# Gate ranks from raw weights in four column strips with the first head's queries turned between them, and score tiles in two halves of 320 columns

## The chip, the cores and the metric

One Trainium2 chip, one of its cores. The metric is the device time of one execution in microseconds, the median of several runs. The engines are PE (TensorE: matrix products and transposes), DVE (VectorE), ACT (ScalarE), POOL (GpSimd) and SP (SyncE, which only issues transfers); each works through its own instructions in order, and semaphores order them against each other.

## What is computed

One inference step of a two-layer mixer with 512 latent and 128 context tokens, width 2048, all in float32. Each layer projects the modulated tokens once, and feeds attention, a short convolution and a gated linear recurrence (GLA) from the pieces:

```python
proj = xn @ w_in
aq, ak, av, ag, ch, cb, cc, cg, gq, gk, gv, gg, glr = jnp.split(proj, SPLIT_POINTS, axis=-1)
q = rmsnorm(aq.reshape(b, t, ATT_HEADS, HEAD_DIM), q_norm_w)
k = rmsnorm(ak.reshape(b, t, ATT_KV_HEADS, HEAD_DIM), k_norm_w)
...
s = jnp.einsum('bqkgd,bskd->bkgqs', qblk.astype(jnp.float32), kf) * scale
p = jax.nn.softmax(s, axis=-1)
...
lr = glr.reshape(b, t, 2, GLA_RANK)
logits = jnp.einsum('btzr,zrk->btzk', lr, a_up) + a_bias
logf = jax.nn.log_sigmoid(logits.astype(jnp.float32)) / GLA_TAU
```

Latent tokens attend to 640 keys: 512 latent and 128 cached ones. There are 8 query heads, and 2 key and value heads. The last 32 columns of `w_in` (`glr`, 2 directions of 16) give the gate ranks.

## The kernel before

**Layout.** Activations lie with features on the 128 partitions and the 640 tokens (`TOK`) along the row; the 2048 features are `KT` = 16 slices. To keep float32 accuracy in fast matmuls, an operand is split into a rounded part and its rest (`x_high`, `x_low`; `high`, `low` for weights, split by ACT and DVE), and each product is three matmuls: high by high, high by low, low by high. Of 640 columns each is made in two halves of `HALF` = 320, since a PSUM bank holds 512; the result starts at column `AT` = 192 of a two-bank tile, so that the halves meet at the bank border.

**Order within a layer.** All order is written out by hand, one stream per engine. First the front: `w_in` in 64 chunks for most projections (L732, L742), with key norms and modulation weights in between. Then `project_quarter(0, 0)` (L767), a first piece of the convolution's projections, which go on in quarters through all attention heads. Then the last prompt turn (`turn_prompt`, L755), whose result ACT stores to the scratch `proj_dram` (L1210), and `gate_ranks` (L693): for each of the 16 slices three products, each in two halves, with 32 weight columns of interest in a block of 128. Its weights came into `raw[1]` by SP (`LR_SLOT`), and DVE splits them (`lr_split`). ACT copies the 32 result rows out (L1298) and stores them.

**The fence.** Between front and heads all engines pass a fence; ACT only once its stores have landed. SP then loads in order: cached key and value tile (L453, L454), tables `cos` and `sin`, the query rows of head 0 into `qraw` (whose memory is named `rstd`, L480), and four partition-swapped pieces into `qturn` (L483). `q_in` counts all five query loads.

**A head.** PE transposes keys and values once per group (L888 to L891), and for each head the raw queries (L925) into `psP[1]`; ACT squares them (L1318), from which DVE gets the norm factors. DVE rotates the queries (L1806 to L1816). PE makes four score tiles of 128 queries by 640 keys (L904) and one small prompt tile (L907); behind each, DVE takes the row maximum (L1845), ACT the exponential (L1329), DVE scales, PE turns the probabilities (L915). Between the tiles PE works on a quarter of a projection. A product with the values (L946) ends the head. For the first head the function `head_products` is called with `begun=True`, since its first quarter has been done.

**The gate logits.** After the heads, and behind a second fence and an output block (`fill`, L973), PE multiplies the stored ranks with `gla_a_up` (L637). `gate_in` loads the ranks (L529) and the two directions' weights (L531) into `aup`, which DVE has cleared before (L1880). It is called twice per layer.

Of the kernel before, what the change touches and what calls it, by code (L numbers as in the profile page):

```python
# [18 lines left out]
F32 = mybir.dt.float32  # L19
F32R = mybir.dt.float32r  # L20
ALU = mybir.AluOpType
# [3 lines left out]
P = 128  # L25
# [114 lines left out]
LR_SLOT = 1  # L140


# [36 lines left out]
mod_step0 mod_step1 mod_half mod_acc mod_summed lr_in lr_split lr_done old_in0 old_in1 x_sq x_acc k_in v_in  # L179
# [18 lines left out]
def backbone(nc, io):  # L198
    with ExitStack() as ctx:
# [42 lines left out]
        with ExitStack() as proj_space:  # L242
# [4 lines left out]
            with ExitStack() as mixers:  # L247
# [15 lines left out]
                lr = lr_att[0:LR_W, :]  # L263
                aup = mx("aup", [LR_W, 2, P])
# [76 lines left out]
        q_back = psP[1][:, 0:TOK]  # L341
# [26 lines left out]
        def _(sp):  # L368
# [46 lines left out]
            for l in range(DEPTH):  # L415
# [10 lines left out]
                for n in range(RING, FRONT_CHUNKS):  # L426
# [7 lines left out]
                    if n == K_LOAD:  # L434

                        sp.wait_ge(s["x_saved"], 16 * SAVES * (l + 1))
# [197 lines left out]
        def _(pe):  # L634
# [190 lines left out]
            for l in range(DEPTH):  # L825
# [50 lines left out]
                pe.wait_ge(s["lr_split"], 2 * l + 2)  # L876
                pe.wait_ge(s["mod_taken"], MOD_CHUNKS + (l + 1) * UNITS + SEED)
                pe.wait_ge(s["k_roped"], (l + 1) * KVH)
                gate_ranks()
                pe.wait_ge(s["prompt_back"], (l + 1) * len(FRONT))  # L880
                for g in range(KVH):
# [12 lines left out]
                    def head_products(h, begun=False):  # L894
# [3 lines left out]
                        def score(i):  # L898

                            pe.wait_ge(s["probs_made"], hd * TT + i + SEED)  # L900
                            if i < TT - 1:
                                for q, x in ((q_high, k_high), (q_high, k_low), (q_low, k_high)):
                                    for part in (slice(0, DEC), slice(DEC, KEYS)):
                                        mm = pe.matmul(psP[1][:, part], q[:, i * P:(i + 1) * P], x[:, part],  # L904
                                                       start=(q is q_high and x is k_high), stop=(q is q_low))
                            else:
                                mm = pe.matmul(psP[1][:, 0:SEQ], qw[:], key[:, g, DEC:TOK], start=True, stop=True)  # L907
# [12 lines left out]
                        else:  # L920
                            pe.wait_ge(s["lr_done"], 2 * l + 2)
                        pe.wait_ge(s["q_in"], hd * 80 + 80)
                        pe.wait_ge(s["probs_made"], hd * TT + SEED)
                        for i in range(TT):
                            mm = pe.transpose(q_back[:, i * P:(i + 1) * P], qraw[:, i * P:(i + 1) * P], ident[:])  # L925
                        mm.then_inc(s["q_rot"], 1)
# [16 lines left out]
                        pe.wait_ge(s["gated"], hd + SEED)  # L943
                        for j in range(KEYS // P):
# [65 lines left out]
                for pr in range(PAIRS):  # L1010
# [5 lines left out]
                    pe.wait_ge(s["gla_lr_in"], gp * 16 * 3 + 16 * 3)  # L1016
# [100 lines left out]
        def _(act):  # L1117
# [59 lines left out]
            for l in range(DEPTH):  # L1177
# [113 lines left out]
                for g in range(KVH):  # L1291
# [3 lines left out]
                    act.activation(k_high[:, 0:DEC], key[:, g, 0:DEC], ACT.Copy).then_inc(s["kv_ready"], 1)  # L1295
# [883 lines left out]
```

## Time and profile before

| | |
|---|---|
| median of 3 runs | 2228.21 us (2228.12 to 2229.08) |
| the profiled execution: time, span | 2229.19 us, 2227.4 us |
| PE busy | 2174.2 us, 98% of the span |
| PE weight loads | 1922.4 us, 86% |
| DVE busy | 1381.7 us, 62% |
| ACT busy | 679.4 us, 31% |
| POOL busy | 186.0 us, 8% |
| granted PE clock, mean | 0.994 |

Weight loads run beside matmuls. A busy PE is one with a matmul in flight. Matmuls are pipelined, so the time that one adds is the distance between starts, not its own duration: a row "x2" that lasts 0.46 us may be followed by the next 0.29 us later. In the trace a plain float32 matmul appears as two instructions. Times are microseconds from the span's start.

### The profile page before, as it was taken

Reading aid. Unit: us, or ns where it says so; the run is one execution under the profiler, and the core shown is the slowest. Engines: PE = TensorE matmul, PEld = TensorE weight load, DVE = VectorE, ACT = ScalarE, POOL = GpSimd, SP = SyncE. Lnnn points to the kernel's source line nnn. Section 1 sums busy time; section 2 is a strip of 40 time slices with the busy share of each in tenths; the row PEclk is TensorE's granted clock in tenths of the full one; section 3 lists DMA queues with packets and bytes.
Section 4 is the critical chain, followed back from the end, with each engine's and each line's share of the span. In section 5 each row is a group of like instructions: output and inputs, shape, how many; then the busy total and the mean of one; then the engine's idle time right before and its main releaser. Section 6 shows DMA issues by size and latency. Waiting matters only on the chain.

```text
span 2227.4 us, 34005 instructions
## 1 busy us (share of the span) xinstructions
PE 2174.2 (98%) x13257; PEld 1922.4 (86%) x13257; DVE 1381.7 (62%) x2701; ACT 679.4 (31%) x1196; POOL 186.0 (8%) x125
## 2 busy tenths in 40 slices
PE   5999999999999999999989999999999999999998
PEld 2578877888999999999988888887799999999998
DVE  5469777986565666666457454555446666666654
ACT  4332222321343333533134222232133333344312
POOL 0000000000000000423321000000000000042331
PEclk9999999999999999999989999999999999999999
DMA  9988587664432333664444645444343333366444
GB/s 353 381 299 299 184 262 229 204 212 138 122 104 79 94 101 111 198 195 134 119 135 141 192 139 177 146 127 129 88 128 91 101 100 101 97 197 196 133 123 146
DMA packets 353200, 362.49 MB, mean 163 GB/s; under 512 B 17062, under 2 KB 259580, under 8 KB 352444
## 3 DMA queue, kind: packets, MB, share of 16 engines
q1 hardware_dynamic: 323536, 317.65, 45.8%
q10 hardware_dynamic: 29548, 43.25, 5.4%
q8 instruction: 78, 1.28, 0.2%
q14 instruction: 38, 0.31, 0.0%
HBM read 301.97 MB, written 58.88 MB: 162 GB/s over the span
## 4 chain that ended last, share of the span: by engine, by line
PE 91%; DVE 3%; ACT 2%; DMA 1%; issue 1%; ACTq 0%; SPq 0%; DVEq 0%
PE psP L732 32%; PE psP L767 20%; PE psP L784 10%; PE psT L742 8%; PE psO L973 5%; PE psP L904 3%; PE psO L946 2%; PE psT L915 2%; PE psO L693 1%; PE psT L973 1%; PE psT L650 1%; PE psO L650 1%; PE psO L797 1%; PE psP L985 1%; PE psP L674 1%
## 5 line engine op out<-in xcount | busy, mean ns | idle before, releaser
L732 PE MATMUL psP<-x_high,high 128*128 128x512 f32 x1024 | 413.1, 403 | 5.6 <-DVE x_low L1689 5.0
L732 PE MATMUL psP<-x_high,low 128*128 128x512 f32 x1024 | 400.7, 391 | 0.0
L732 PE MATMUL psP<-x_low,high 128*128 128x512 f32 x1024 | 400.7, 391 | 0.0
L1634 DVE SCALAR_TENSOR_TENSOR macc<-mraw,cond,macc 128x384 f32<-128x384 f32 (+1 forms) x960 | 389.7, 480 | 0.0
L1175 ACT ACTIVATE high<-raw 128x1024 fp32r<-128x1024 f32 x128 | 135.4, 1058 | 520.8 <-PE psT L742 507.0
L732 PEld LDWEIGHTS psP<-x_high,high 128*128 128x128 f32 x1024 | 193.2, 189 | 65.3 <-issue 24.0
L767 PE MATMUL psP<-x_high,high 128*128 128x320 f32 x1024 | 243.3, 319 | 0.5 <-issue 0.5
L767 PE MATMUL psP<-x_high,low 128*128 128x320 f32 x1024 | 233.3, 309 | 0.0
L767 PE MATMUL psP<-x_low,high 128*128 128x320 f32 x1024 | 232.7, 308 | 0.0
L732 PEld LDWEIGHTS psP<-x_high,low 128*128 128x128 f32 x1024 | 193.1, 189 | 41.6
L732 PEld LDWEIGHTS psP<-x_low,high 128*128 128x128 f32 x1024 | 193.5, 189 | 39.0 <-issue 1.9
L1652 DVE TENSOR_TENSOR low<-raw,high 128x1024 fp32r<-128x1024 f32 x128 | 163.9, 1281 | 100.0 <-ACT high L1175 100.0
L767 PEld LDWEIGHTS psP<-x_low,high 128*128 128x128 f32 x1024 | 171.0, 188 | 0.0
L767 PEld LDWEIGHTS psP<-x_high,low 128*128 128x128 f32 x1024 | 170.9, 188 | 0.0
L767 PEld LDWEIGHTS psP<-x_high,high 128*128 128x128 f32 x1024 | 167.1, 189 | 1.5 <-issue 0.7
L973 PE MATMUL psO<-x_high,high 128*128 128x320 f32 x704 | 134.9, 313 | 4.7 <-DVE low L1904 4.7
L2082 POOL MEMSET cu<- 128x643 f32 x2 | 1.3, 636 | 1645.8 <-DVEq L359 1645.8
L784 PE MATMUL psP<-second_high,high 128*128 128x320 f32 x512 | 116.9, 309 | 0.2 <-DVE low L1587 0.2
L973 PEld LDWEIGHTS psO<-x_high,high 128*128 128x128 f32 x704 | 109.2, 188 | 8.8 <-issue 7.4
L784 PE MATMUL psP<-second_low,high 128*128 128x320 f32 x512 | 116.6, 309 | 0.0
L784 PE MATMUL psP<-second_high,low 128*128 128x320 f32 x512 | 116.6, 309 | 0.0
L1624 DVE TENSOR_SCALAR macc<-mraw,cond 128x384 f32<-128x384 f32 (+1 forms) x64 | 19.7, 350 | 156.2 <-PE psO L797 144.7
(312 smaller groups left out, 3508.1 us busy)
## 6 DMA issues: line engine op xcount, KB each, us to landing
raw<-in_w_in_dram SPq DMA_DIRECT2D x128, 512.0 KB, 4.7
wmod<-in_w_mod_dram SPq DMA_DIRECT2D x32, 1024.0 KB, 9.5
mraw<-in_w_mod_dram SPq DMA_DIRECT2D x64, 512.0 KB, 4.3
mraw<-in_w_mod_dram SPq DMA_DIRECT2D x32, 1024.0 KB, 7.0
raw<-in_w_in_dram SPq DMA_DIRECT2D x32, 1024.0 KB, 6.1
raw<-in_w_out_dram SPq DMA_DIRECT2D x64, 512.0 KB, 4.4
old<-x_scratch SPq DMA_DIRECT2D x64, 320.0 KB, 3.0
proj_scratch<-stage ACTq DMA_DIRECT2D x64, 256.0 KB, 3.2
```

Of the source, the lines that this page charges most:

```text
L650: mm = pe.matmul(mod_ps[t % 2][32 * k:32 * k + 2, :], cond[:, q * KT // 4 + k, :], wmod[q][:, k, :], start=(q == 0), stop=(q == 3), skip_g ...
L732: mm = pe.matmul(latent_ps[m], w[:, kk, cols], x[:, k, 0:DEC], start=(k == 0 and w is whole and x is x_high), stop=(k == KT - 1 and w is r ...
L742: mm = pe.matmul(prompt_ps, x[:, k, DEC:TOK], w[:, kk, :], start=(k == 0 and w is whole and x is x_high), stop=(k == KT - 1 and w is rest))
L767: mm = pe.matmul(psP[0][:, AT + half * HALF:AT + (half + 1) * HALF], w[slot][:, k, :], x[:, k, half * HALF:(half + 1) * HALF], start=(k == ...
L784: mm = pe.matmul(out[:, AT + half * HALF:AT + (half + 1) * HALF], w[slot][:, at + k, :], x[:, k, half * HALF:(half + 1) * HALF], start=(k ...
L904: mm = pe.matmul(psP[1][:, part], q[:, i * P:(i + 1) * P], x[:, part], start=(q is q_high and x is k_high), stop=(q is q_low))
L915: mm = pe.transpose(psT[:, j * P:(j + 1) * P], probs[i % 2][:, j * P:(j + 1) * P], ident[:])
L946: pe.matmul(psO[:, 0:DEC], v[:, j, :], x[:, j, :], start=(j == 0 and v is vals_high and x is probs_high), stop=(j == KEYS // P - 1 and v i ...
L973: mm = pe.matmul(out[:, AT + half * HALF:AT + (half + 1) * HALF], w[slot][:, at + k, :], x[:, k, half * HALF:(half + 1) * HALF], start=(k ...
L1175: act.activation(ring(high, n), ring(raw, n), ACT.Copy).then_inc(s["chunk_cast"], 1)
L1634: m = dve.scalar_tensor_tensor(acc[:, v, 0:width], mraw[hf][:, k, 0:width], c, acc[:, v, 0:width], ALU.mult, ALU.add)
L1652: dve.tensor_tensor(ring(low, n), ring(raw, n), ring(high, n).bitcast(F32), ALU.subtract)\
```

## The change

Four things are done in the same edit.

1. The gate rank weights are loaded raw, 32 columns wide, into a place of their own (`lr_w`) in the middle of the front, and are not split. The ranks are plain float32 matmuls against `x_high` and `x_low`. The output goes to four strips of 32 PSUM partitions: slice k + n to strip n. Each strip holds the partial sum of four slices. The four are not added there: all 128 rows are copied, stored and loaded again, and `aup` holds four copies of its 32 rows, so that the gate logits' contraction over 128 rows adds them.
2. The ranks are made in two halves (slices 0 to 7, 8 to 15), and head 0's query turn, taken out of `head_products` as `query_turn`, stands between them. ACT makes head 0's squares ahead of its copy of the ranks. The wait for `lr_done` moves from the head's start to its value product.
3. The score tile goes to `score_ps`, which starts at column 192, in two halves of 320 columns instead of 512 and 128. Row maximum and exponential read it there.
4. SP's load of the second convolution weight slot no longer waits for the rank weights' split.

```diff
+            with ExitStack() as rank_space:
+                ps_("below", [P, KT * MOD_N + 72], F32, rank_space)
+                lr_w = ps_("lr_w", [P, KT, LR_W], F32, rank_space)
...
-        q_back = psP[1][:, 0:TOK]
+        q_back, score_ps = psP[1][:, 0:TOK], psP[1][:, AT:AT + KEYS]
...
                     if n == K_LOAD:
+                        sp.dma_start(lr_w[:], w_in[:, :, T_LR * P:T_LR * P + LR_W]).then_inc(s["lr_in"], 16)
...
                 sp.wait_ge(s["chunk_split"], (l + 1) * FRONT_CHUNKS)
-                sp.dma_start(raw[LR_SLOT][:, :, 0:LR_W], w_in[:, :, T_LR * P:T_LR * P + LR_W]).then_inc(s["lr_in"], 16)
-                sp.wait_ge(s["lr_split"], 2 * l + 2)
                 conv_weights(1, 0)
...
-                    sp.dma_start(lr, proj_dram[T_LR, 0:LR_W, :]).then_inc(s["gla_lr_in"], 16)
-                    for z in range(2):
-                        sp.dma_start(aup[z * RANK:(z + 1) * RANK, z, :], io["gla_a_up"][l, z][:, pr * P:(pr + 1) * P])\
-                            .then_inc(s["gla_lr_in"], 16)
+                    sp.dma_start(lr, proj_dram[T_LR]).then_inc(s["gla_lr_in"], 16)
+                    for at in range(0, P, LR_W):
+                        for z in range(2):
+                            sp.dma_start(aup[at + z * RANK:at + (z + 1) * RANK, z, :],
+                                         io["gla_a_up"][l, z][:, pr * P:(pr + 1) * P]).then_inc(s["gla_lr_in"], 16)
...
-            def gate_ranks():
-                for k in range(KT):
-                    for w, x in ((high, x_high), (high, x_low), (low, x_high)):
+            def gate_ranks(first, last):
+                for k in range(first, last, LR_STRIPS):
+                    for x in (x_high, x_low):
                         for half in range(2):
-                            mm = pe.matmul(lr_ps[:, half * HALF:(half + 1) * HALF], w[LR_SLOT][:, k, :],
-                                           x[:, k, half * HALF:(half + 1) * HALF],
-                                           start=(k == 0 and w is high and x is x_high), stop=(k == KT - 1 and w is low))
-                mm.then_inc(s["lr_done"], 1)
+                            part = slice(half * HALF, (half + 1) * HALF)
+                            for n in range(LR_STRIPS):
+                                mm = pe.matmul(lr_ps[n * LR_W:(n + 1) * LR_W, part], lr_w[:, k + n, :],
+                                               x[:, k + n, part].bitcast(F32), start=(k == 0 and x is x_high),
+                                               stop=(k == KT - LR_STRIPS and x is x_low), skip_group_check=True)
+                if last == KT:
+                    mm.then_inc(s["lr_done"], 1)
+
+            def query_turn(hd):
+                pe.wait_ge(s["q_in"], hd * 80 + 80)
+                pe.wait_ge(s["probs_made"], hd * TT + SEED)
+                for i in range(TT):
+                    mm = pe.transpose(q_back[:, i * P:(i + 1) * P], qraw[:, i * P:(i + 1) * P], ident[:])
+                mm.then_inc(s["q_rot"], 1)
...
-                pe.wait_ge(s["lr_split"], 2 * l + 2)
+                pe.wait_ge(s["lr_in"], 32 * l + 16)
                 pe.wait_ge(s["mod_taken"], MOD_CHUNKS + (l + 1) * UNITS + SEED)
                 pe.wait_ge(s["k_roped"], (l + 1) * KVH)
-                gate_ranks()
+                gate_ranks(0, KT // 2)
+                query_turn(l * HEADS)
+                gate_ranks(KT // 2, KT)
...
-                                    for part in (slice(0, DEC), slice(DEC, KEYS)):
-                                        mm = pe.matmul(psP[1][:, part], q[:, i * P:(i + 1) * P], x[:, part],
+                                    for part in (slice(0, HALF), slice(HALF, KEYS)):
+                                        mm = pe.matmul(score_ps[:, part], q[:, i * P:(i + 1) * P], x[:, part],
...
+                    def query_squares(hd):
+                        act.wait_ge(s["q_rot"], hd + 1 + SEED)
...
                     if g == 0:
+                        query_squares(hd0)
                         act.wait_ge(s["lr_done"], 2 * l + 1)
-                        act.activation(stage[0][0:LR_W, :], lr_ps[0:LR_W, :], ACT.Copy).then_inc(s["lr_done"], 1)
+                        act.activation(stage[0][:], lr_ps, ACT.Copy).then_inc(s["lr_done"], 1)
...
-                dve.tensor_copy(high[LR_SLOT][:, :, 0:LR_W], raw[LR_SLOT][:, :, 0:LR_W]).then_inc(s["lr_split"], 1)
-                dve.wait_ge(s["lr_split"], 2 * l + 1)
-                dve.tensor_tensor(low[LR_SLOT][:, :, 0:LR_W], raw[LR_SLOT][:, :, 0:LR_W],
-                                  high[LR_SLOT][:, :, 0:LR_W].bitcast(F32), ALU.subtract).then_inc(s["lr_split"], 1)
...
-                        dve.wait_ge(s["lr_done"], 2 * l + 1)
```

PE's queue in layer 0, around the ranks, before (`psO<-x_high,high` are the ranks, `psT<-ident,r_b` the last prompt turn, `psP<-x_low,high` the projection):

```order
L767 MATMUL psP<-x_high,low 128x320 x2
L755 MATMUL psT<-ident,r_b 128x128 [waits prompt_back,prompt_taken]
L755 MATMUL psT<-ident,r_b 128x128 x3
L693 MATMUL psO<-x_high,high 128x320 [waits k_roped,mod_taken,lr_split]
L693 MATMUL psO<-x_high,high 128x320
L693 MATMUL psO<-x_low,high 128x320 x2
L693 MATMUL psO<-x_high,low 128x320 x2
```

and the same place of the changed kernel, to the key and value turns (`psT<-ident,xf`, `psT<-ident,ck`); `psP<-ident,rstd` is the query turn:

```order
L768 MATMUL psT<-ident,r_b 128x128 [waits prompt_back,prompt_taken]
L768 MATMUL psT<-ident,r_b 128x128 x3
L697 MATMUL psO<-x_high,lr_w 32x320 [waits k_roped,mod_taken,lr_in]
L697 MATMUL psO<-x_high,lr_w 32x320 x7
L697 MATMUL psO<-x_low,lr_w 32x320 x8
L697 MATMUL psO<-x_high,lr_w 32x320 x8
L697 MATMUL psO<-x_low,lr_w 32x320 x8
L708 MATMUL psP<-ident,rstd 128x128 [waits probs_made,q_in]
L708 MATMUL psP<-ident,rstd 128x128 x4
L697 MATMUL psO<-x_high,lr_w 32x320 x8
L697 MATMUL psO<-x_low,lr_w 32x320 x8
L697 MATMUL psO<-x_high,lr_w 32x320 x8
```

Before, 96 matmuls stood in one piece; now 32 stand ahead of the wait for `q_in` and 32 behind it.

SP's queue between the front and the heads, before:

```order
L395 DMA raw<-in_w_in_dram 128x2x512 [waits chunk_split]
L459 DMA raw<-in_w_in_dram 128x16x128 [waits split0,chunk_split]
L448 DMA xf<-proj_scratch 128x640 [waits kv_turned]
L466 DMA raw<-in_w_in_dram 128x16x32 [waits chunk_split]
L459 DMA raw<-in_w_in_dram 128x16x128 [waits split1,lr_split]
L453 DMA ck<-in_cache_k_dram 128x128 [waits phase_over]
```

The rank weight load (L466) is gone from here, and the load behind it waits for `chunk_split` alone. At the gate logits the changed kernel's SP queue reads:

```order
L530 DMA lr_att<-proj_scratch 128x640 [waits aup_clear]
L533 DMA aup<-in_gla_a_up_dram 16x128 x8
L545 DMA states<-in_state_gla_dram 128x128 [waits phase_over]
L545 DMA states<-in_state_gla_dram 128x128
```

where there were two `aup` loads, and the first load had 32 rows.

## Rows read from the trace of the kernel before

**Rows 1.** The page, chain of work that ended last, shares of the span by engine
```profile
PE 91%; DVE 3%; ACT 2%; DMA 1%; issue 1%; ACTq 0%; SPq 0%; DVEq 0%
```

**Rows 2.** Timeline of PE, layer 0, ranks to first head: start us, us, engine, instruction
```profile
555.19 0.54 PE L693 MATMUL psO<-x_high,high 128*128 128x320 f32 x2
...
569.57 0.71 PE L891 MATMUL psT<-ident,xf 128*128 128x128 f32 x5
...
570.82 0.54 PE L767 MATMUL psP<-x_high,high 128*128 128x320 f32 x2
```

**Rows 3.** Timelines of SP, ACT and DVE there; last: DMA issues, median us to landing
```profile
551.90 0.37 SPq L459 DMA_DIRECT2D raw<-in_w_in_dram  x1
...
556.16 0.39 ACTq L1210 DMA_DIRECT2D proj_scratch<-r_a  x1
...
559.68 0.34 SPq L453 DMA_DIRECT2D ck<-in_cache_k_dram  x1
...
567.65 0.29 DVE L1806 TENSOR_SCALAR qw<-rstd,vecs 128x128 f32<-128x128 f32 x1 [2.74 <-DMA qturn<-proj_scratch]
...
proj_scratch<-r_a ACTq DMA_DIRECT2D x16, 256.0 KB, 2.5
```

**Rows 4.** Timeline of PE, conditioning matmuls in four column strips
```profile
102.59 1.90 PE L650 MATMUL psT<-wmod,cond 128*2 128x512 f32 x16
...
106.01 1.04 PE L650 MATMUL psT<-wmod,cond 128*2 128x512 f32 x8
```

**Rows 5.** Windows (us; PE, PEld, DVE, ACT, POOL busy; PEclk; DMA); then timeline of PE
```profile
1148.00:1150.00 2.00, 1.42 (x6) 1.42 (x7) 0.46 (x3) 0.00 (x0) 0.00 (x0) 0.52 0.00 0
...
1160.00:1162.00 2.00, 2.00 (x7) 1.51 (x6) 1.97 (x5) 1.15 (x2) 0.00 (x0) 0.57 0.71 152
...
1156.10 0.76 PE L732 MATMUL psP<-x_high,high 128*128 128x512 f32 x1 [5.02 <-DVE x_low L1689]
```

**Rows 6.** Timelines of DVE and PE, layer 0, head 0
```profile
575.76 0.17 DVE L1826 TENSOR_SCALAR qv<-qb 128x5 f32<-128x5 f32 x1 [1.56 <-ACT probs L1318]
...
576.86 0.51 PE L767 MATMUL psP<-x_high,high 128*128 128x320 f32 x2
...
577.21 0.46 PE L767 MATMUL psP<-x_low,high 128*128 128x320 f32 x2
...
580.76 0.56 PE L904 MATMUL psP<-k_high,q_high 128*128 128x512 f32 x2 [0.16 <-ACT probs L1329]
```

**Rows 7.** Timeline of PE, one score tile of a later query tile
```profile
590.67 0.46 PE L767 MATMUL psP<-x_high,low 128*128 128x320 f32 x2
...
590.96 0.45 PE L904 MATMUL psP<-k_high,q_high 128*128 128x512 f32 x2
...
591.25 0.51 PE L904 MATMUL psP<-k_low,q_high 128*128 128x512 f32 x2
...
591.60 0.51 PE L904 MATMUL psP<-k_high,q_low 128*128 128x512 f32 x2
...
591.94 0.71 PE L915 MATMUL psT<-ident,probs 128*128 128x128 f32 x5
```

**Rows 8.** Timelines of SP and PE, first gate logits; last: DMA issues
```profile
884.65 0.33 SPq L529 DMA_DIRECT2D lr_att<-proj_scratch  x1
...
885.01 0.89 SPq L531 DMA_DIRECT2D aup<-in_gla_a_up_dram  x2
...
888.93 1.12 PE L637 MATMUL psP<-lr_att,aup 32*128 32x512 f32 x2
...
aup<-in_gla_a_up_dram SPq DMA_DIRECT2D x8, 8.0 KB, 2.1
```

**Rows 9.** Timelines of DVE and PE, layer 1, same places as rows 2, 3, 6
```profile
1630.80 0.28 DVE L1806 TENSOR_SCALAR qw<-rstd,vecs 128x128 f32<-128x128 f32 x1 [1.86 <-DMA qturn<-proj_scratch]
...
1634.40 0.54 PE L767 MATMUL psP<-x_high,high 128*128 128x320 f32 x2
...
1644.32 0.57 PE L904 MATMUL psP<-k_high,q_high 128*128 128x512 f32 x2 [0.16 <-ACT probs L1329]
```

More of the change, by code:

```diff
@@ L902, in score @@
                                 for q, x in ((q_high, k_high), (q_high, k_low), (q_low, k_high)):
-                                    for part in (slice(0, DEC), slice(DEC, KEYS)):
-                                        mm = pe.matmul(psP[1][:, part], q[:, i * P:(i + 1) * P], x[:, part],
+                                    for part in (slice(0, HALF), slice(HALF, KEYS)):
+                                        mm = pe.matmul(score_ps[:, part], q[:, i * P:(i + 1) * P], x[:, part],
                                                        start=(q is q_high and x is k_high), stop=(q is q_low))
                             else:
-                                mm = pe.matmul(psP[1][:, 0:SEQ], qw[:], key[:, g, DEC:TOK], start=True, stop=True)
+                                mm = pe.matmul(score_ps[:, 0:SEQ], qw[:], key[:, g, DEC:TOK], start=True, stop=True)
                             mm.then_inc(s["scored"], 1)
@@ L919, in head_products @@
                             project_quarter(0, 0, n)
[L920 to L926, printed above, removed]
+                            query_turn(hd)
                         project_quarter(0, 1, n)
@@ L1295, in _ @@
                     act.activation(k_high[:, 0:DEC], key[:, g, 0:DEC], ACT.Copy).then_inc(s["kv_ready"], 1)
+                    def query_squares(hd):
+                        act.wait_ge(s["q_rot"], hd + 1 + SEED)
+                        for i in range(TT):
+                            act.activation(q_squares[:, i * P:(i + 1) * P], q_back[:, i * P:(i + 1) * P], ACT.Square,
+                                           accum_out=qb[:, i:i + 1]).then_inc(s["q_sq"], 1)
                     if g == 0:
+                        query_squares(hd0)
                         act.wait_ge(s["lr_done"], 2 * l + 1)
[L1298 removed]
+                        act.activation(stage[0][:], lr_ps, ACT.Copy).then_inc(s["lr_done"], 1)
                         act.wait_ge(s["lr_done"], 2 * l + 2)
[L1300 removed]
+                        act.dma_start(proj_dram[T_LR], stage[0][:]).then_inc(s["lr_in"], 16)
                     act.wait_ge(s["kv_turned"], kv + 1 + SEED)
@@ L1313, in _, with head_scalars @@
                                   newv[:]).then_inc(s["kv_stored"], 16)
-                    def head_scalars(h):
+                    def head_scalars(h, squared=False):
                         hd = h + hd0
-                        act.wait_ge(s["q_rot"], hd + 1 + SEED)
-                        for i in range(TT):
-                            act.activation(q_squares[:, i * P:(i + 1) * P], q_back[:, i * P:(i + 1) * P], ACT.Square,
-                                           accum_out=qb[:, i:i + 1]).then_inc(s["q_sq"], 1)
+                        if not squared:
+                            query_squares(hd)
                         act.wait_ge(s["q_r"], hd + 1)
@@ L1328, in prob @@
                             act.wait_ge(s["prob_turned"], hd * TT + max(i - 1, 0) + SEED)
-                            act.activation(probs[i % 2][:, 0:width], psP[1][:, 0:width], ACT.Exp,
+                            act.activation(probs[i % 2][:, 0:width], score_ps[:, 0:width], ACT.Exp,
                                            bias=nm[:, i:i + 1], scale=qs[:, i:i + 1], accum_out=sums[:, i:i + 1])\
@@ L1362, in head_scalars @@
                         take_tile(1)
-                    with act.Fori(0, GROUP) as h:
+                    if g == 0:
+                        head_scalars(0, squared=True)
+                    with act.Fori(1 if g == 0 else 0, GROUP) as h:
                         head_scalars(h)
```

17 lines of the change are left out of this document (9 added, 8 removed).

## The prediction

> **What bounds the kernel now.** I read the page's chain of work first: 91% of the span is PE's own work, so time is won or lost where PE's own stream gets shorter or where PE comes to stand still [rows 1]. Then the timeline of the stretch between the front projection and the first attention head, PE alone. In layer 0 the gate ranks (L693) begin at 555.19, the key and value turns (L891) at 569.57, the first head's projection (L767) at 570.82 [rows 2]. The ranks are 96 matmuls of 320 columns at about 0.147 us (a pair takes 0.29, [rows 7]): 14.1 us of the stream.
>
> Next, what the other engines and queues do beneath those 14 us [rows 3]. The last prompt store leaves ACT's queue at 556.16; ACT passes the fence only when it has landed, and SP's first load behind the fence is issued at 559.68. Then come two cache tiles, two tables, the query row tile and its four turned parts, one behind another, and DVE's first query step (L1806) begins at 567.65, released by the last of them. So the query of head 0 is there 12.5 us after the ranks begin. Now that costs nothing: PE needs it only at 570.3. The 14.1 us of ranks are the cover of this load chain, and that is what the reader should carry into the next part.
>
> **Part 1: the ranks in strips.** 64 matmuls per layer, four at a time in four column strips. The nearest rows are the conditioning matmuls (L650): the same strips, the same 128 rows, plain float32, 512 columns, but 2 weight columns. Each shows as two instructions; 16 take 1.90 us and 8 take 1.04 [rows 4], so 8 more cost 0.86 us, which is a set of four matmuls. For 320 columns that is 0.54 us a set, 16 sets a layer: 8.6 us, 4.3 a half. Weight loads have 32 columns here instead of 2; what they add is not in the rows. I take 4.4 us a half. Upper bound, if the strips do not run together: 64 times 0.54 is 34 us.
>
> By the Trainium skill, page "TensorE: Matmul & The Clock Gate" (Part 3, The mechanism), weight loads pass running matmuls only where the row group differs, and all four strips share their rows; with that page's 27 ns for 32 columns, an estimate of 1.7 us more for each half. No row here shows it.
>
> **Part 2: the query turn between the halves.** It waits for all of q_in, and in PE's queue the second half of the ranks, the key and value turns and the head's projection stand behind it. The first half ends at 555.2 + 4.4 = 559.6. The query is due at 567.65 as before, or sooner: SP used to issue a 1 MB weight load at 551.90, held back until the rank weights were split, and the prompt store ran beside it and took 3.5 us to the fence, where the median of such stores is 2.5 [rows 3]. That load now goes out earlier. I take 0.9 us for this (bounds 0 and 1.3): query at 566.75. So PE stands still for about 7 us, and the shorter ranks win nothing: the load chain sets the restart.
>
> What follows the restart: five query turns and seven key and value turns, 1.5 us (the ranks end near 569.35, 96 times 0.1475 after 555.19, and L767 begins at 570.82, [rows 2]), and 4.4 us of ranks, 5.9 us at full clock. The clock will not be full, I think. In the longest gap of this trace the granted clock reads 0.52 (the 1.2 GHz level) in the window 1148 to 1150, where PE does thin work with pauses; then PE idles 5.02 us, restarts at 1156.10, and in the window 1160 to 1162 the clock still reads 0.57, so it rose near 1161.7, some 5.4 us after the restart [rows 5]. With the same here, the first 5.4 us do 2.7 us of work: L767 begins at 566.75 + 5.4 + 3.2 = 575.35, 4.5 us later than before. With the clock full it would be 572.65.
>
> Part of that comes back. Before, DVE waited 1.56 us for ACT's query squares, and score 0 with it; the squares are now made long before. Score 1 started at 580.76, released by ACT's first exponential [rows 6]. From the end of the key and value turns (570.28, [rows 2]) to that release there lie 10.5 us on ACT and DVE; less the 1.56, 8.9. The new turns end at 575.3, so score 1 starts at 584.2; PE itself would be there at 583.3. **Layer 0: +3.4 us.** In layer 1 the query came 3.60 us before L767 (1630.80, 1634.40), in layer 0 3.17 us [rows 2, 3, 9], so its shift is 0.4 smaller: **+3.0 us**. Its score 1 was at 1644.32, with the same 0.16 us wait [rows 9], so the tail is the same.
>
> **Part 3: the score halves.** 8 heads, 4 tiles, 2 layers: 64 tiles of three pairs, 512 + 128 columns before, 320 + 320 now. In a steady head the pair before the score starts at 590.67 and the score at 590.96; the next pairs at 591.25 and 591.60, the probability turns at 591.94 [rows 7]. So a 512 + 128 pair costs 0.35 behind another such pair, and all three 0.98 us. A pair of 320s costs 0.293; three are 0.88. That saves 0.10 a tile. Where a projection follows instead of a turn, its first pair takes 0.35 instead of 0.29 (576.86 to 577.21, [rows 6]): 0.06 more, for tile 0 of each head. Both heads of the chain above already hold their own tile 0, so 48 tiles at 0.10 and 14 at 0.16: **-7.0 us**. No wait stands between the rows of a steady head, so PE's shorter stream counts in full. Bounds: 0, and 0.057 on all 192 pairs, 10.9 us.
>
> A rule speaks against this term. The Trainium skill, same page (Wait — 56ns, not 53.3ns?), puts the gap between matmuls at N / 2.4 GHz + 2.5 ns: 271.6 ns for either pair, so the halves would win nothing. The 0.35 of the rows does not agree with it, and the measured pairs go into the sum.
>
> **Part 4: the low-rank weights in four copies.** SP issues nine loads instead of three before the gate logits (L637). Before: first at 884.65, the next two from 885.01 in 0.89 us, 0.445 each; logits at 888.93, straight behind a fill [rows 8]. Now the last of eight starts at 888.1 and lands 2.1 us later, at 890.2: PE stops for **1.3 us**, in both layers, +2.6. The state loads behind them in SP's queue come later too; I take them as covered by the later logits. The second pair's loads start 20 us before their use and cost nothing; the eight cost nothing there. The contraction over 128 rows instead of 32 streams the same columns. If small loads landed at once, 0; if as slowly as 4 us, 3.2 a layer.
>
> **Part 5, at nothing:** the two split steps that DVE loses, which PE does not wait for; the 256 KB rank weight load moved into the front, one SP issue under PE's front work; the 128-row copy and store instead of 32 rows.
>
> **Sum.** +3.4 + 3.0 - 7.0 + 2.6 = +2.0 us. The profiled execution took 2229.19 us, span 2227.4, 1 us above the median of 2228.21; on the median the sum gives **2230.2**. No change that a measurement of this kernel can tell begins at about 0.2%, 4.5 us.
>
> **The rivals.**
> *The clock holds, or the query comes much sooner.* Part 2 then ends at 572.65 for L767, and score 1 at 570.28 to 572.6 shifted: 572.6 + 8.9 = 581.5, +0.7 us instead of +3.4, and +0.3 in layer 1. Sum -3.4; with logits that do not stall, or scores at their upper bound, -6 to -7: 2221 to 2224. For it: PE idles 7 us, not longer, and only one gap bears the clock out. Against: that gap was shorter. 0.28, about half of it beyond 4.5 us below.
> *The strips do not overlap at 32 columns* (slower). Half the ranks then take 17 us: the first half covers the query, the second ends at 589.4 and L767 starts near 590.9, 20 us late; with 1.6 won back at the score it is +18 a layer: 2265. Against: [rows 4]. It decides once a set costs more than about 0.8 us instead of 0.54. 0.06.
> *The small loads land late* (a dearer wait than the one I forecast). If each takes 4 us from issue to landing instead of 2.1, the logits wait 3.2 us a layer, +3.8 in all: 2234. Their transfers share the queue with a 320 KB load ahead of them, which speaks for it; the median of eight speaks against. 0.14.
> *The halves win nothing* (the page's rule): pairs of equal column count, 640, would take equal time, as they would if the 0.06 us were lost elsewhere. Sum +9.0: 2237. 0.07, since [rows 7] speak against it.
> My own case: 0.45.
>
> **How the numbers follow.** Range 2222 to 2237: from the middle of the first rival to the fourth, leaving the strips' failure and the best sums out. Faster by over 0.2%: half or more of the first rival and the upper tail of Part 3, 0.24. Slower: strips, late loads above the bound, no gain of the halves, and a slice of my own case, 0.26. Between, 0.50.
>
> **What would show it.** A PE gap of about 7 us ahead of the query turn in both layers, released by the turned query parts; a granted clock of 0.5 in the windows after it and rank matmuls there at twice the spacing; each layer's rank matmuls busy for 4 to 5 us a half at full clock; score 1 of head 0 some 3 us later than before, counted from the ranks' start; score tiles of 0.88 us from first matmul to the turn; a wait of about 1.3 us ahead of the first gate logits in each layer on the eighth small load. I am wrong if the query arrives by 562, if the clock stays full through the gap, or if the score tile keeps 0.98.

## The result and the profile after

The changed kernel took 2232.96 us (median of 16 runs, 2229.47 to 2237.83), the kernel before 2228.28 us on the same chip (16 runs): ratio 1.0023, 95% interval 1.0016 to 1.0030. That is 3.6 to 6.7 us slower, 5.1 in the middle, against a forecast of 2.0.

The profiled execution took 2229.47 us, which is the shortest of its 16 runs. I therefore read places and mechanisms from it, and sizes also from a second profile of the same kernel (experiment 1, 2232.88 us, near the median). First the page of the changed kernel: engines, and the chain that ended last.

```profile
PE 2156.2 (97%) x13321; PEld 1902.7 (85%) x13321; DVE 1378.4 (62%) x2697; ACT 669.2 (30%) x1188; POOL 186.4 (8%) x125
...
PE 22%; DVE 2%; ACT 1%; issue 1%; DMA 1%; SPq 0%; ACTq 0%; DVEq 0%
```

The chain's shares add up to 27% of the span; the view follows the chain over a much shorter way than in [rows 1], so the two can't be set against each other. That PE is busy 97% of the span still says where to look: at the places where it stands still. Its waits in the changed kernel (total us, times, longest):

```profile
PE psP L708 <- DMA qturn<-proj_scratch: 12.2, 2, 6.5
...
PE psP L919 <- ACT probs L1346: 2.9, 2, 1.4
...
PE psP L639 <- DMA aup<-in_gla_a_up_dram: 2.7, 2, 1.8
```

The first and the last of these are new. The middle one stood at 0.16 a layer before [rows 6]. Next, PE's timeline in layer 0 from the ranks (L697) past the turn (L708) to the first head (L780), the counterpart of [rows 2]:

```profile
553.87 1.28 PE L697 MATMUL psO<-x_high,lr_w 128*32 128x320 f32 x16
...
554.97 1.26 PE L697 MATMUL psO<-x_low,lr_w 128*32 128x320 f32 x16
...
564.90 1.33 PE L708 MATMUL psP<-ident,rstd 128*128 128x128 f32 x5 [6.52 <-DMA qturn<-proj_scratch]
566.16 2.36 PE L697 MATMUL psO<-x_high,lr_w 128*32 128x320 f32 x16
568.29 1.61 PE L697 MATMUL psO<-x_low,lr_w 128*32 128x320 f32 x16
569.73 1.25 PE L697 MATMUL psO<-x_high,lr_w 128*32 128x320 f32 x16
...
572.27 0.71 PE L906 MATMUL psT<-ident,xf 128*128 128x128 f32 x5
572.73 0.54 PE L780 MATMUL psP<-x_high,high 128*128 128x320 f32 x2
...
582.33 0.56 PE L919 MATMUL psP<-k_high,q_high 128*128 128x320 f32 x2 [1.44 <-ACT probs L1346]
```

Each row of 16 instructions is a group of eight matmuls. The groups begin 1.10, 1.08 and 1.07 us apart, so a half of the ranks, four groups, is 4.3 us. Then PE stands 6.52 us. The first group after the restart takes 2.13 us until the next, twice as long, the second 1.44, and the third has the old pace. The windows show the clock there (us; PE, PEld, DVE, ACT, POOL busy; PEclk; DMA), as [rows 5] did:

```profile
559.00:561.00 2.00, 0.00 (x0) 0.00 (x0) 0.00 (x0) 0.00 (x0) 0.00 (x0) 1.00 0.92 283
561.00:563.00 2.00, 0.00 (x0) 0.00 (x0) 0.84 (x2) 0.00 (x0) 0.00 (x0) 0.80 0.88 272
563.00:565.00 2.00, 0.10 (x1) 0.10 (x2) 0.12 (x1) 0.00 (x0) 0.00 (x0) 0.50 0.98 275
...
567.00:569.00 2.00, 2.00 (x20) 0.76 (x16) 1.34 (x3) 0.67 (x6) 0.00 (x0) 0.50 0.56 134
569.00:571.00 2.00, 2.00 (x36) 0.87 (x32) 0.00 (x0) 0.00 (x0) 0.00 (x0) 0.99 0.00 0
```

The granted clock falls to 0.50, the 1.2 GHz level, while PE stands idle, and is back at 2.4 GHz about 4 us after the restart at 564.90. What the query waits for stands on ACT, SP and DVE, the counterparts of [rows 3]:

```profile
554.66 0.39 ACTq L1221 DMA_DIRECT2D proj_scratch<-r_a  x1
...
557.11 0.34 SPq L458 DMA_DIRECT2D ck<-in_cache_k_dram  x1
...
564.88 0.28 DVE L1820 TENSOR_SCALAR qw<-rstd,vecs 128x128 f32<-128x128 f32 x1 [2.49 <-DMA qturn<-proj_scratch]
```

From the issue of the prompt store (554.66) to SP's first load behind the fence (557.11) there are 2.45 us (3.52 before), and the query is there 11.0 us after the ranks begin (12.5 before). Behind it, the first head's exponential on ACT:

```profile
580.01 1.28 ACT L1346 ACT_TABLE_LOAD   x1 [2.89 <-DVE nm L1861]
581.31 0.89 ACT L1346 ACTIVATE probs<-psP,nm,qs 128x640 f32<-128x640 f32 x1
```

The table load of 1.28 us starts only after DVE's last maximum step (`nm`), so all of it lies open: from the end of `nm` to the start of the exponential there are 1.37 us. In the kernel before it started at 578.43, after the step before the maximum (`qs`), and 0.33 us lay open. In the changed kernel head 0 stands outside ACT's loop over the heads; the 14 heads inside it still have the load behind `qs`. A steady score tile and the gate logits, on PE's timeline, counterparts of [rows 7] and [rows 8]:

```profile
592.33 0.46 PE L919 MATMUL psP<-k_high,q_high 128*128 128x320 f32 x2
...
593.21 0.71 PE L930 MATMUL psT<-ident,probs 128*128 128x128 f32 x5
...
888.89 1.12 PE L639 MATMUL psP<-lr_att,aup 128*128 128x512 f32 x2 [1.76 <-DMA aup<-in_gla_a_up_dram]
```

And the nine small loads ahead of these logits, on SP's timeline:

```profile
882.76 0.33 SPq L530 DMA_DIRECT2D lr_att<-proj_scratch  x1
883.13 3.67 SPq L533 DMA_DIRECT2D aup<-in_gla_a_up_dram  x8
```

The tile takes 0.88 us where it took 0.98, and the logits wait 1.76 us for the eighth load; in layer 1 they wait 0.9.

### The profile page after: what moved, and what is told of

It reads as the page before. It is cut to its first block and busy times, and to the rows that moved or that the text cites. A ratio compares the mean times of both kernels' runs of the same rounds, so it can differ in the third digit from the quotient of the medians.

```text
span 2227.6 us, 34115 instructions
## 1 busy us (share of the span) xinstructions
PE 2156.2 (97%) x13321; PEld 1902.7 (85%) x13321; DVE 1378.4 (62%) x2697; ACT 669.2 (30%) x1188; POOL 186.4 (8%) x125
## 5 line engine op out<-in xcount | busy, mean ns | idle before, releaser
L780 PE MATMUL psP<-x_high,high 128*128 128x320 f32 x1024 | 242.6, 318 | 0.5 <-issue 0.5
L780 PE MATMUL psP<-x_high,low 128*128 128x320 f32 x1024 | 233.3, 309 | 0.0
L780 PE MATMUL psP<-x_low,high 128*128 128x320 f32 x1024 | 232.9, 309 | 0.0
L780 PEld LDWEIGHTS psP<-x_low,high 128*128 128x128 f32 x1024 | 171.2, 188 | 0.0
L780 PEld LDWEIGHTS psP<-x_high,low 128*128 128x128 f32 x1024 | 170.9, 188 | 0.0
L780 PEld LDWEIGHTS psP<-x_high,high 128*128 128x128 f32 x1024 | 167.5, 188 | 0.8 <-issue 0.6
L984 PE MATMUL psO<-x_high,high 128*128 128x320 f32 x704 | 134.9, 313 | 6.2 <-DVE low L1917 6.2
L984 PEld LDWEIGHTS psO<-x_high,high 128*128 128x128 f32 x704 | 109.2, 188 | 10.4 <-issue 9.0
```

What stands on the lines that cost most here:

```text
L780: mm = pe.matmul(psP[0][:, AT + half * HALF:AT + (half + 1) * HALF], w[slot][:, k, :], x[:, k, half * HALF:(half + 1) * HALF], start=(k == ...
L984: mm = pe.matmul(out[:, AT + half * HALF:AT + (half + 1) * HALF], w[slot][:, at + k, :], x[:, k, half * HALF:(half + 1) * HALF], start=(k ...
```

## The experiments

Each ratio is to the kernel before on the same chip. Experiments 1 to 4 shared one chip (before: 2227.39 us, 13 runs), 5 to 8 another (2228.26 us, 27 runs).

**1. The changed kernel again**, no edit.

> The changed kernel once more, beside the others on the same chip. My theory (PE stands still before the query turn, the clock falls, and how long it stays low differs from run to run): 2229 to 2236 us, and the executions lie wider apart than those of the kernel before; the mean granted clock is lower where the time is longer, near 0.988 at the slow end and 0.992 at the fast end. Rival (the change costs a fixed 4 to 5 us, and the spread is chance): times within 1 to 2 us of 2233, and no tie between clock and time.

2233.47 us, ratio 1.0025 (1.0014 to 1.0036). The eight runs lie between 2230.19 and 2236.07 us, the 13 of the kernel before between 2226.62 and 2229.47; the longest has the lowest mean clock (0.989) and the shortest one of the highest (0.992), as expected. Its layer 1 on PE's timeline, and then two windows there:

```profile
1629.13 1.33 PE L708 MATMUL psP<-ident,rstd 128*128 128x128 f32 x5 [5.67 <-DMA qturn<-proj_scratch]
1630.39 2.36 PE L697 MATMUL psO<-x_high,lr_w 128*32 128x320 f32 x16
1632.53 2.36 PE L697 MATMUL psO<-x_low,lr_w 128*32 128x320 f32 x16
1634.66 1.50 PE L697 MATMUL psO<-x_high,lr_w 128*32 128x320 f32 x16
...
1647.51 0.57 PE L919 MATMUL psP<-k_high,q_high 128*128 128x320 f32 x2 [1.44 <-ACT probs L1346]
```

```profile
1633.00:1635.00 2.00, 2.00 (x20) 0.79 (x16) 0.00 (x0) 0.00 (x0) 0.00 (x0) 0.50 0.00 0
1635.00:1637.00 2.00, 2.00 (x32) 0.72 (x24) 0.00 (x0) 0.00 (x0) 0.00 (x0) 0.96 0.00 0
```

Here two groups and part of a third run at the low level: the clock came back some 6 us after the restart. In the shortest run the same layer had waited as long (5.69 us) and was back about 3 us after. The gap hardly differs; how long the clock stays low does, and with it the time from run to run. The same shows where no edit reaches: behind the wait of 5.02 us in [rows 5] the clock came back 5.6 us after the restart (1156.10 to about 1161.7), and behind the same wait of 5.01 us in experiment 1 after 3.0 (1157.67 to about 1160.7):

```profile
1160.00:1162.00 2.00, 2.00 (x9) 1.62 (x8) 2.00 (x2) 1.78 (x4) 0.53 (x1) 0.83 0.95 356
```

**2. The halves alone**, on the kernel before:

```diff
-for part in (slice(0, DEC), slice(DEC, KEYS)):
-    mm = pe.matmul(psP[1][:, part], ...
+for part in (slice(0, HALF), slice(HALF, KEYS)):
+    mm = pe.matmul(score_ps[:, part], ...      # score_ps = psP[1][:, AT:AT + KEYS]
...                                              # maximum and exponential read score_ps
```

> The kernel before with the score tiles in two halves of 320 columns and nothing else. My theory: 48 + 14 tiles at 0.10 and 0.16 us, and two more tiles 0 that the wait for the squares does not hide: 6.5 to 7.3 us faster than before, about 2221.3. Rival (equal columns take equal time): 2228, no change.

2221.30 us, ratio 0.9969 (0.9957 to 0.9981): 4.2 to 9.6 us faster, 6.9 in the middle (6.1 between the medians). From head 0's to head 7's value matmuls in layer 0 there are 269.58 us where before had 272.75; seven heads at 0.46 should save 3.22, and 3.17 was saved.

**3. Everything but the halves**, on the changed kernel:

```diff
-score_ps = psP[1][:, AT:AT + KEYS]
+score_ps = psP[1][:, 0:KEYS]
-for part in (slice(0, HALF), slice(HALF, KEYS)):
+for part in (slice(0, DEC), slice(DEC, KEYS)):
```

> The changed kernel with its score tiles in 512 + 128 columns again, so the ranks, the query turn and the four copies alone. My theory: 7 us slower than the changed kernel, 2237 to 2243, that is 9 to 14 us slower than before. Rival (the halves win nothing, or the ranks' part is worth a gain): 2226 to 2233.

2240.75 us, ratio 1.0060 (1.0046 to 1.0074), 10.2 to 16.5 us slower, 13.4 in the middle, where the terms gave 9.0. The granted clock of its profiled run also drops behind the logits' wait:

```profile
895.00:897.00 2.00, 2.00 (x6) 0.97 (x5) 0.00 (x0) 0.79 (x1) 0.00 (x0) 0.50 0.92 296
```

From there to the second pair's logits it needs 77.23 us, the kernel before 75.16. So a wait of 1.8 us at the logits can cost some 2 us more behind it. In the profiles of the changed kernel (both) the clock held there, and that stretch took 75.12 and 75.46 us.

**4. The ranks in one piece**, the query turn back in front of its head, and ACT's squares back in its loop over the heads:

```diff
-gate_ranks(0, KT // 2)
-query_turn(l * HEADS)
-gate_ranks(KT // 2, KT)
+gate_ranks(0, KT)
...
-    query_squares(hd0)                          # ACT, ahead of its copy of the ranks
...
-    head_scalars(0, squared=True)
-with act.Fori(1 if g == 0 else 0, GROUP) as h:
+with act.Fori(0, GROUP) as h:
```

> The changed kernel, but the 16 slices of the ranks in one piece and the query turn behind the key and value turns, as before. My theory: ranks end near 8.7 us after they begin, PE waits only 1 to 3 us for the query instead of 6.5, the ranks' second half stands ahead of the wait and at full clock; first head 5 to 8 us earlier per layer: 12 us faster than the changed kernel, about 2221 (2216 to 2225), and close executions if the clock stays full. Rival (the place of the query turn does not matter, the loads behind the fence or the strips themselves set the time): 2230 to 2236.

2220.15 us, ratio 0.9964 (0.9951 to 0.9978). PE's timeline in layer 0, then a window there, then ACT's timeline:

```profile
562.43 1.26 PE L697 MATMUL psO<-x_low,lr_w 128*32 128x320 f32 x16
...
563.90 0.71 PE L904 MATMUL psT<-ident,xf 128*128 128x128 f32 x5
566.53 0.77 PE L708 MATMUL psP<-ident,rstd 128*128 128x128 f32 x5 [1.93 <-DMA qturn<-proj_scratch]
...
576.61 0.56 PE L917 MATMUL psP<-k_high,q_high 128*128 128x320 f32 x2
```

```profile
568.00:570.00 2.00, 2.00 (x10) 2.00 (x9) 1.90 (x5) 1.99 (x11) 0.00 (x0) 0.50 1.09 349
```

```profile
574.28 1.28 ACT L1343 ACT_TABLE_LOAD   x1 [1.87 <-DVE qs L1847]
```

With all ranks and the key and value turns ahead of it, the same query costs 1.93 us of waiting instead of 6.66. Score 1 starts 22.3 us after the last prompt turn, in experiment 1 29.2, in the kernel before 25.9. The difference is 6.9 us in layer 0 and 7.2 in layer 1, against 13.6 us between this kernel and the changed one (ratios: 0.0061). About 1 us of it in each layer is not the place of the turn: ACT's table load is behind `qs` again, and the exponential starts 0.35 us after `nm` and not 1.37. The clock falls here too, behind the wait of 1.93 us, but for a shorter time.

Against experiment 2, which has the halves and no strips, this kernel is only 0.0005 (1 us) faster, and the intervals overlap. Score 1 comes 3.7 and 4.1 us earlier than in the kernel before, but part of that is lost again behind the heads, 2.6 us in the waits at the logits alone. So with the turn in its old place the strips win nothing that these runs can tell; with the turn between their halves they lose.

**5. Work in the gap**, 27 matmuls that nothing reads, ahead of the turn:

```diff
 gate_ranks(0, KT // 2)
+pe.wait_ge(s["probs_made"], l * HEADS * TT + SEED)
+for _ in range(27):
+    pe.matmul(psP[1][:, 0:DEC], high[1][:, 0, :], x_high[:, 0, 0:DEC], start=True, stop=True)
 query_turn(l * HEADS)
```

> The changed kernel with 27 extra matmuls of 512 columns, about 6.1 us, in PE's wait between the first half of the ranks and the query turn; their output is overwritten and belongs to nothing. My theory (the clock falls in the gap and the restart pays for it at 1.2 GHz): the granted clock stays full there, the second half takes 4.4 us instead of 5.4 to 6.5, 2 to 3 us per layer come back, so 4 to 6 us faster than the changed kernel, 2228 to 2230, and executions closer together, mean clock 0.994. Rival (only the wait itself costs): no faster than 2233, or slower by what the filler overhangs.

2230.43 us, ratio 1.0012 (1.0003 to 1.0022). PE's timeline, and then two windows:

```profile
559.06 6.46 PE L895 MATMUL psP<-x_high,high 128*128 128x512 f32 x27
565.36 0.71 PE L708 MATMUL psP<-ident,rstd 128*128 128x128 f32 x5
...
570.61 0.27 PE L907 MATMUL psT<-ident,ck 128*128 128x128 f32 x1
...
1972.21 0.82 PE L987 MATMUL psO<-x_high,high 128*128 128x320 f32 x4 [1.87 <-DVE low L1920]
```

```profile
567.00:569.00 2.00, 2.00 (x37) 0.93 (x31) 1.66 (x3) 0.50 (x4) 0.00 (x0) 1.00 0.80 197
888.00:890.00 2.00, 2.00 (x5) 1.10 (x4) 0.00 (x0) 0.46 (x1) 0.00 (x0) 0.50 0.84 255
```

The clock stays at 1.00, and from the turn to the first cache turn PE needs 5.25 us; experiment 1 needed 7.3 in layer 0 and 8.2 in layer 1. So the low clock costs 2.1 and 2.9 us in the two layers of experiment 1. Of those 5.0 us the ratios show 2.9 (0.0013), with an uncertainty as large. In layer 1 little of it can be seen even in the profile: there the query came 12.3 us after the ranks began, where experiment 1 had 10.2, so PE stood 1.43 us behind the 27 matmuls, and score 1 came only 0.8 us earlier than in experiment 1 (2.5 in layer 0). SP's issue of the `cos` table took 1.48 us there and not 0.43, and the parts landed later; whether the extra matmuls have to do with it stays open. In the profiled run the clock fell at two other places: behind the logits' wait in layer 0 (window 888 to 890), and in layer 1 behind a wait of 1.87 us for a split (L987, last row; 0.75 in the kernel before). From the first to the second pair's logits that run needs 76.75 and 77.59 us in the two layers, experiment 1 75.46 and 75.78: 3.1 us given back.

**6. One copy instead of four.** It leaves out three of the four copies, so the gate logits take the first strip's partial sum alone and the outputs are not those of the step; only its time is of use.

```diff
-LR_LOADS = 1 + 2 * LR_STRIPS
+LR_LOADS = 3
-for at in range(0, P, LR_W):
+for at in (0,):
```

> The changed kernel with two of the eight loads of low-rank weights in each gate load; it leaves out three of the four copies, so the gate logits take the first strip's partial sum alone. My theory: the waits of 1.8 and 0.9 us ahead of the first gate logits vanish, and the later loads of that stage come 2.7 us earlier, 2.7 us in all: 2229.5 to 2231.5. Where the stage loses more than the two waits, as the fills behind seem to (6.3 us of waits on weight splits against 4.7 before), up to 5 us: 2228. Rival (the extra small loads are hidden): 2233.

2230.12 us, ratio 1.0008 (0.9999 to 1.0017). No wait stands ahead of the logits any more. The four copies cost the difference to experiment 1, 0.0017 or 3.8 us. That is uncertain by some 3 us, so it agrees with the 2.6 us of their two waits and shows no more.

**7. The ranks in one piece and the copies loaded early**: experiment 4, and a tile of its own for all pairs' copies, loaded during the front.

```diff
+if n in range(40, 40 + PAIRS):
...
+    for at in range(0, P, LR_W):
+        for z in range(2):
+            sp.dma_start(aups[at + z * RANK:at + (z + 1) * RANK, n - 40, z, :],
+                         io["gla_a_up"][l, z][:, (n - 40) * P:(n - 39) * P]).then_inc(s["aups_in"], 16)
...
```

> The ranks in one piece with the query turn behind the key and value turns, as in e4, and the four copies of the low-rank weights loaded in the front into a place of their own, so that the gate logits wait for one load only. My theory: e4's 2220.2 less the stall and what follows it, 2.7 to 4 us: 2216 to 2217.5. Rival (the sixteen small loads in the front delay its weight chunks, or the stall is not what the stage loses): 2219 to 2222.

2215.98 us, ratio 0.9947 (0.9934 to 0.9961), the fastest kernel here with experiment 9: 0.0022 or 4.9 us better than the halves alone, 3.8 better than experiment 4 (the middles of overlapping intervals). The logits follow a fill without a wait, and PE's wait for the query is short, once a layer (PE's timeline; then its waits: total, times, longest):

```profile
879.98 1.02 PE L645 MATMUL psP<-lr_att,aups 128*128 128x512 f32 x2
```

```profile
PE psP L714 <- DMA qturn<-proj_scratch: 3.2, 2, 1.9
```

**8. The turn waits for the raw query alone**, not for its four turned parts:

```diff
-pe.wait_ge(s["q_in"], hd * 80 + 80)
+pe.wait_ge(s["q_in"], hd * 16 + 16)        # the turned parts count on qt_in, for DVE
```

> The changed kernel, but the query turn waits only for the raw query rows, not for the four turned pieces, which have a semaphore of their own. My theory (the load chain behind the fence sets the restart): the query turn starts 1.5 to 2.5 us sooner, the gap shrinks from 6.5 to about 4.5 us in layer 0, and 3 to 5 us are won in all: about 2229. Rival (the transfers all end together, since the later ones share the queues): the turn starts less than 0.7 us sooner, 2232.

2229.84 us, ratio 1.0009 (1.0000 to 1.0018). PE's timeline:

```profile
564.22 1.33 PE L708 MATMUL psP<-ident,rstd 128*128 128x128 f32 x5 [5.52 <-DMA rstd<-proj_scratch]
```

The raw query itself comes late: 5.52 us of the gap stay. What the parts add is 1.1 us in this layer and 0.6 in the other, so the expected step of 1.5 to 2.5 us did not come, though the time of 2229 nearly did. Score 1, counted from the last prompt turn, comes 1.7 and 2.0 us earlier than in experiment 1; in layer 1 0.6 of that is the wait, and the rest is a clock that came back 3.4 us after the restart and not 6.0.

**9. Experiments 7 and 8 together** (a chip with before at 2228.50 us, 9 runs).

> e7 with the query turn waiting for the raw query rows alone, as in e8. In e7 PE waited 3.2 us in two places for the turned pieces, and in layer 0 the granted clock fell for a short stretch behind that wait. My theory: the raw rows land 0.7 to 1 us sooner, so 1.5 to 2 us of the waits go, and the score that follows now waits for DVE, whose own query steps still need the turned pieces; 0 to 2 us faster than e7, 2214 to 2216. Rival (DVE's rotated queries set the first score anyway): 2216, no change.

2215.86 us, ratio 0.9940 (0.9926 to 0.9953), not to be told from experiment 7. Waits of PE:

```profile
PE psP L923 <- DVE vals_low L1814: 3.3, 2, 1.6
...
PE psP L714 <- DMA rstd<-proj_scratch: 1.6, 2, 0.9
```

The wait moved: PE turns the query earlier and then stands at the first score for DVE's split of the values.

## Why the prediction came out as it did

The time fell inside the range and on the forecast side of zero, 3 us above the forecast. The forecast steps were there, but the sum left 3 us out, and the width of the range covered them; "within 0.2%" was the likeliest of three, and the ratio of 1.0023 lies just beyond it. The account below is made in the profile of experiment 1 against that of before: spans 2231.1 and 2227.4, +3.7 us.

**Part 1, right.** 4.4 us a half was forecast and 4.3 measured. The Trainium skill, page "TensorE: Matmul & The Clock Gate" (Part 3, The mechanism), would have added an estimated 1.7 us a half, since strips that share their rows can't load weights under running matmuls; the 1.08 us for each 16 instructions do not agree: they are 0.54 for a set of four matmuls, what the rows of the conditioning matmuls gave without such a term.

**Part 2, right in kind and in sum.** The gap was forecast at about 7 us, released by the turned parts, and was 6.52 and 5.69 us (6.66 and 5.67 in experiment 1). The store passed the fence 1.07 us sooner; 0.9 was taken for the whole chain, and the query came 11.0 us after the ranks' start (11.2 in experiment 1) where 11.6 was forecast. The clock was forecast to stay low for 5.4 us after the restart and stayed low for 3 to 6. That figure came from one gap, misread twice: by [rows 5] it is 5.6 us (1156.10 to 1161.7), and that gap is not the longest of the trace, since PE waits 13.66 us at its start. Errors inside cancel, which is luck: the low clock cost 1.4 to 2.9 us where 2.7 was taken; the query came up to half a microsecond sooner than taken; and from the key and value turns to score 1 there lie 9.6 us (572.73 to 582.33) where 8.9 was taken, because ACT's table load, for the most part under DVE's row maximum before, now comes after it. Counted from the last prompt turn, score 1 of experiment 1 is 3.3 us later than before in layer 0 and 3.2 in layer 1, where +3.4 and +3.0 were forecast. Experiment 5 says how much of that is the clock (2.1 and 2.9 us). With the turn in its old place (experiment 4) score 1 is not later but 3.7 and 4.1 us earlier than before; about 1 us of that turnabout is the table load, the rest is the place of the turn.

**Part 3, right.** 0.88 us a tile, 3.17 us over seven heads, and 6.9 us in all (4.2 to 9.6) for a forecast of 7.0. The Trainium skill, same page (Wait — 56ns, not 53.3ns?), has a gap that depends on columns alone and would give nothing for the halves; the 0.98 and 0.88 us don't agree with it.

Parts 2 and 3 together, from the last prompt turn to head 7's value matmuls, were to give -0.1 us in layer 0 and -0.5 in layer 1. They gave -0.21 and -0.30.

**Part 4, the size right, a consequence missing.** The logits wait 1.7 and 0.9 us in experiment 1, 2.6 in all, as forecast (1.3 in each). The missing step is that the clock can fall behind a wait of this kind. It did so in experiments 3 and 5, in layer 0, where 2.1 and 1.6 us were lost up to the next pair, and not in the four other profiles that have the wait. The prediction saw the clock at risk in the long gap only. The trace of the kernel before had a warning: among the conditioning matmuls at its start, with waits of 1.40 and 1.58 us (47.26 and 49.88), the clock fell too (window, as [rows 5]):

```profile
50.00:52.00 2.00, 2.00 (x9) 0.30 (x2) 1.97 (x3) 1.66 (x4) 0.00 (x0) 0.50 1.05 386
```

Since the profiles of the changed kernel itself don't have the drop at the logits, how often its other runs have it stays open. Experiment 3 lies 4.4 us above its terms, but the changed kernel lies 3.1 and 3.6 above its own (ratios 1.0023 and 1.0025), so that excess is for the most part not this drop.

**What the sum left out.** The terms give +2.1 in that profile, the span grew by 3.7. Of the rest, 1.3 us stand at the very end. The DMA engines' mean busy share and GB/s in the last 4.4 us, 40 slices, in the kernel before and then in the changed one:

```profile
DMA  9999979989979899989899999997997700000000
GB/s 410 447 372 410 447 298 447 410 335 447 447 298 559 335 410 447 372 335 484 335 373 521 372 410 410 410 484 298 410 484 298 298 0 0 0 0 0 0 0 0
```

```profile
DMA  9999999999999999999310000000000000000000
GB/s 410 410 372 447 372 372 410 410 373 410 410 447 447 410 447 372 372 410 410 112 38 37 0 37 37 0 37 37 37 0 37 37 0 0 0 0 0 0 0 0
```

Before, all engines end the output stores together. After, they end, and for 1.3 us a trickle of about 25 GB/s goes on, a sixteenth of the rate, as if one of the 16 engines had more left than the others. This trickle is in all the profiles with strips except that of experiment 5, and not in those of before and experiment 2. Experiment 5 has the same data transfers as the changed kernel, so their number alone doesn't decide it; the cause stays open.

The other pieces are -0.6 us ahead of the first ranks and +0.8 in the stages between. That +0.8 hides a gain and a loss. From the wait of 5 us in [rows 5] to layer 1's last prompt turn PE needs 460.75 us in experiment 1 and 462.30 in the kernel before, 1.5 less, for the clock came back sooner there. So the other stages grew by 2.4: 0.3 and 0.6 from the first to the second pair's logits (75.46 and 75.78 us, before 75.16 and 75.18), 0.4 and 1.0 in the output blocks behind them, the rest in small pieces. One stage differs by 1.5 us between profiles where no edit explains it, so this growth is not shown to be the change's. In it PE's waits for one kind of weight split (L973 before, L984 after) have grown from 4.7 to 6.3 us. They are 4.7 in experiment 2, 5.8 in experiment 6 and 6.4 in experiment 7, which has neither the eight late loads nor the turn between the halves; so it is something else that comes with the strips, and it stays open. By the ratio the growth is 5.1 us, by the medians 4.7; some 1.5 us of the difference to 3.7 come from the two profiled executions, of which that of before was 0.9 us above its median and that of experiment 1 0.6 below.

**The rivals.** "The clock holds" is false, though experiment 5 forced it. Strips that don't overlap, loads that land late, and halves that win nothing are each refuted by a row above. The time given for the first of these, 2265, is a slip: its own terms, 2228.2 with 18 us twice, -7.0 and +2.6, make about 2260.

## What to carry to other kernels

Ahead of moving a step that waits on a load chain, count what covered the chain: 14 us of ranks hid the query. Putting the wait in the middle of the shortened stream, and head 0 outside ACT's loop with it, made the kernel 13.6 us slower than the same stream uncut. Where the work over a load chain gets shorter than the chain, the wait is what is left: 1.93 us even with all the ranks ahead of it. Price an idle gap of TensorE with its low-clock stretch behind it, here 1.4 to 2.9 us for gaps of 5.7 to 6.7. When weights are needed in several copies, load them during a long stage: eight small loads cost SP 3.7 us of issue, and early they cost nothing that showed.

## What the hardware did that I had not expected

The clock came back about 3 us after the restart in one profile and about 6 in another, in the same place after gaps of 5.69 and 5.67 us; and 3.0 and 5.6 us after the restart behind the gap of 5.0 us ahead of layer 1's front.

Short waits can be followed by the low level as well, and their length does not tell which. It followed waits of 1.84 and 1.94 us at the logits (experiments 3 and 5), of 1.93 and 1.86 at the query (experiments 4 and 7; 0.50 in the windows 568 to 570 and 567 to 569) and of 1.87 at a weight split (experiment 5). It did not follow waits of 1.71 to 1.76 at the logits (both profiles of the changed kernel, experiment 4), nor of 1.79 to 1.87 at weight splits of the same kind (the changed kernel, experiments 3, 4, 7, 8 and 9).

Four strips of plain float32 weights with 32 columns run side by side like strips with 2: 64 instructions of 320 columns in 4.3 us. ACT's table load of 1.28 us stood behind the wait for `qs` in the heads of the loop and behind the later wait for `nm` in the head outside it. And the output stores ended with a trickle of 1.3 us at a sixteenth of the rate, in eight of the nine profiles with strips.
